# A layer kernel on one core: a second fold in its Fourier mixing, output projection and top-k in one stage, context rows gathered as quarter rows

## The reference

```
x = x + gate1 * (concat(fourier(p), retention(p)) @ w_out)    # p = modulated RMSNorm(x) @ w_in
h2 = RMSNorm(x) * (1 + scale2) + shift2
aff = softmax(h2 @ w_router)                                  # 16 experts
gates, idx = top_k(aff.T, cap)                                # 128 latent and 32 context tokens an expert
y = (silu(h2[idx] @ w_gate) * (h2[idx] @ w_up)) @ w_down      # 2816 hidden columns an expert
x = x + gate2 * scatter_add(gates * y)
```

## Time and profile before

| what | us |
|---|---|
| median of 3 runs (3186.18 to 3187.97) | 3187.58 |
| profiled execution | 3188.28 |
| its span | 3186.5 |
| PE busy in the span | 2995.0 (94%) |
| DVE, ACT, POOL busy | 1039.8, 692.7, 323.3 |
| mean granted clock of PE, as a share | 0.969 |

### The profile page before, as it was taken

The page is one execution under the profiler, slowest core; times in us unless marked ns, Lnnn a source line. Parts: engine busy times, 40 slices in busy tenths (PEclk is TensorE's granted clock), DMA queues, the critical chain, the costliest instruction groups (busy, mean ns, idle before and its releaser), DMA issues. The chain is left out here.

```text
span 3186.5 us, 50737 instructions
## 1 busy us (share of the span) xinstructions
PE 2995.0 (94%) x20563; PEld 2622.7 (82%) x20563; DVE 1039.8 (33%) x1977; ACT 692.7 (22%) x1158; POOL 323.3 (10%) x436
## 2 busy tenths in 40 slices
PE   5899998897499999999999999999999999999994
PEld 1899997586488888888888888888888888888883
DVE  4333331222533333333333333333333333333322
ACT  4222221233112121212212121212212121212212
POOL 1243330122000000000000000000000000000002
PEclk9999999898699999999999999999999999999997
DMA  9311102343577786868687786968787696968684
GB/s 372 99 41 35 40 12 66 106 145 134 166 245 248 232 289 202 295 207 287 229 275 251 228 293 198 295 207 290 228 273 255 224 294 199 294 208 292 220 270 147
DMA packets 483301, 668.17 MB, mean 210 GB/s; under 512 B 14689, under 2 KB 418993, under 8 KB 480050
## 3 DMA queue, kind: packets, MB, share of 16 engines
q1 hardware_dynamic: 476978, 644.45, 60.4%
q0 software_dynamic: 6144, 20.98, 2.8%
HBM read 633.39 MB, written 31.98 MB: 209 GB/s over the span
## 5 line engine op out<-in xcount | busy, mean ns | idle before, releaser
L1393 PEld LDWEIGHTS psG<-X,rawW 128*128 128x128 f32 x5632 | 772.5, 191 | 73.0 <-issue 72.1
L1393 PE MATMUL psG<-X,rawW 128*128 128x160 f32 x5632 | 815.0, 303 | 1.1 <-DVE X L1493 0.7
L1393 PE MATMUL psU<-X,rawW 128*128 128x160 f32 x5632 | 793.8, 299 | 0.0
L1393 PEld LDWEIGHTS psU<-X,rawW 128*128 128x128 f32 x5632 | 774.6, 190 | 0.0
L1474 ACT ACTIVATE wD_hi<-rawW 128x1024 fp32r<-128x1024 f32 x352 | 352.6, 1049 | 1314.1 <-PE psP L1412 1286.5
L1521 DVE TENSOR_TENSOR wD_lo<-rawW,wD_hi 128x1024 fp32r<-128x1024 f32 x352 | 415.2, 1220 | 560.0 <-ACT wD_hi L1474 560.0
L1526 DVE TENSOR_TENSOR hf<-sg,psU 128x320 f32<-128x320 f32 x176 | 85.9, 488 | 939.8 <-issue 825.7
L1407 PE MATMUL psS<-wD_hi,hid_hi 128*128 128x512 f32 x704 | 240.4, 423 | 0.0
L1407 PE MATMUL psS<-wD_hi,hid_lo 128*128 128x512 f32 x704 | 221.1, 395 | 0.0
L1407 PE MATMUL psS<-wD_lo,hid_hi 128*128 128x512 f32 x704 | 218.1, 391 | 0.0
L1550 POOL DMA_INDIRECT xgS<-xn,gi x16 | 16.4, 1024 | 1759.6 <-DVE gi L1518 1723.1
(11 more groups left out here) (219 smaller groups left out, 2720.7 us busy)
## 6 DMA issues: line engine op xcount, KB each, us to landing
rawW<-in_w_gate SPq DMA_DIRECT2D x176, 1024.0 KB, 7.8
rawW<-in_w_up SPq DMA_DIRECT2D x176, 1024.0 KB, 11.0
rawW<-in_w_down SPq DMA_DIRECT2D x176, 1024.0 KB, 5.3
wm<-in_w_mod SPq DMA_DIRECT2D x24, 1024.0 KB, 9.0
raw<-in_w_in SPq DMA_DIRECT2D x32, 192.0 KB, 2.5
rawc<-catT SPq DMA_DIRECT2D x10, 512.0 KB, 6.1
acc<-x SPq DMA_DIRECT2D x10, 512.0 KB, 2.7
xn<-xn SPq DMA_DIRECT2D x10, 512.0 KB, 4.1
```

Source lines behind the costliest of these rows:

```text
L1393: mm = pe.matmul(out[:, f, 0:C], w[:, k, f * P:(f + 1) * P], X[:, odd, k, :], start=(k == 0), stop=(k == NK - 1), skip_group_check=True)
```

## The change

In C the position DFT is folded a second time: `V` holds even and odd combinations of 256 positions, the tables shrink, and the matmuls into `pa` and `pb` have 256 columns; the one-row and single-column matmuls go, and a matmul of two columns (`edge`) gives what the fold leaves over. PE's loop is written out. SP loads `w_out`, `w_router` and half of the first two `catT` tiles during C.

D and E become one stage. PE transposes the residual stream without its norm; ACT copies it in one piece (`x1T`); the logits are made from `wrA` (router weight times scale) with 32 stationary columns in four column groups (`partials`), added up by `fold4`, and corrected by the norm's factor and a shift row (`srow`). The residual add moves from POOL to DVE, the scaling to `xn` from DVE to ACT. The softmax is done tile by tile (`affinity`), and DVE's rounds for the latent tokens start between tile 8's and tile 9's work.

The ring's first loads are issued at the start of F. In F the context rows are 128 quarter rows (`xgP`, `ysP` 128x256, on views `xn2q`, `accq`). The first expert's transposes go to eight banks (`first_x`), scaled by ACT and DVE in turn; later experts transpose `xgP` in one step only (`CTX_K`), and DVE then scales eight 128x32 pieces.

```diff
+                            for k in KO:
+                                sp.dma_start(rawo[:, k, :], io["w_out"][0, k * P:(k + 1) * P, :]).then_inc(d_raw[k], 16)
+                            for t in range(2):
+                                sp.dma_start(rawc[:, t, HALF[0], :], catv[:, HALF[0], t * P:(t + 1) * P]
+                                             ).then_inc(d_early[t], 16)
+                            sp.dma_start(wr[:], io["w_router"][0].rearrange("(k p) e -> p k e", p=P)).then_inc(d_wr, 16)
...
                     over_groups(sp, body)
                     store(H - 1)
-                    sp.wait_ge(c_out, 16 + 16 * H)
...
-                            pe.matmul(pa[:], Z[:, n, 0, :], pcos[:, n, 0:512], start=(n == 0), stop=False)
-                            pe.matmul(pb[:], Z[:, n, 1, :], psin[:, n, :], start=(n == 0), stop=(n == 3))
+                            pe.matmul(pa[:, at], Z[:, n, 0, :], pcos[:, t, odd, :], start=(t == 0), stop=(t == 1))
+                            mm = pe.matmul(pb[:, at], Z[:, n, 1, :], psin[:, t, odd, :], start=(t == 0), stop=(t == 1))
+                        mm.then_inc(c_lat, 1)
                         pe.wait_ge(c_rowc, g + 1)
-                        pe.matmul(pa[:], Zrow[:], palt[:, 0:512], start=False, stop=True)
-                        for n in range(4):
-                            pe.matmul(pm[:, 256:257], Z[:, n, 0, :], pcos[:, n, 512:513], start=(n == 0), stop=False)
-                        pe.matmul(pm[:, 256:257], Zrow[:], palt[:, 512:513], start=False, stop=True)
...
+                        act.wait_ge(c_lat, g + 1)
+                        act.activation(Bs[:].rearrange("p a k -> p (a k)"), pb[:], ACT.Copy).then_inc(c_bs, 1)
+                        waits(act, (c_rowc, g + 1), (c_out, 16 * (g + 1)))
+                        act.activation(yf[:, 512:513], zc[:, 1:2], ACT.Copy, scale=N_S ** -0.5)
                         act.wait_ge(c_pos, g + 1)
...
+                        dve.tensor_tensor(V[:, 0, 0, :], Ue[:, 0:256], Ue[:, 512:256:-1], ALU.add).then_inc(c_part, 1)
+                        dve.tensor_tensor(V[:, 0, 1, :], Ue[:, 0:256], Ue[:, 512:256:-1], ALU.subtract)
+                        dve.tensor_tensor(V[:, 1, 0, 1:256], Uo[:, 1:256], Uo[:, 511:256:-1], ALU.subtract)
+                        dve.tensor_tensor(V[:, 1, 1, 1:256], Uo[:, 1:256], Uo[:, 511:256:-1], ALU.add)
+                        dve.tensor_copy(V[:, 1, 1, 0:1], Uo[:, 256:257])
+                        dve.tensor_copy(edge[:, 0:1], Ue[:, 256:257])
+                        waits(dve, (c_part, 2 * g + 1))
+                        dve.tensor_reduce(part2[:].unsqueeze(2), V[:, 0, 0, :].rearrange("p (m a) -> p a m", a=2), AX.X,
+                                          ALU.add).then_inc(c_part, 1)
+                        waits(dve, (c_part, 2 * g + 2))
+                        dve.scalar_tensor_tensor(edge[:, 1:2], part2[:, 0:1], Ue[:, 256:257], part2[:, 1:2],
+                                                 ALU.add, ALU.subtract).then_inc(c_fold, 1)
...
+                        waits(dve, (c_bs, g + 1), (c_rowc, g + 1), (c_out, 16 * (g + 1)))
+                        dve.scalar_tensor_tensor(As[:], alt[:], zc[:, 0:1], pa[:, 0:256], ALU.mult, ALU.add).then_inc(c_as, 1)
+                        dve.tensor_tensor(yf[:, 1:512:2], pa[:, 256:512], Bs[:, 1, :], ALU.add)
+                        dve.tensor_tensor(yf[:, 1023:512:-2], pa[:, 256:512], Bs[:, 1, :], ALU.subtract)
+                        waits(dve, (c_as, g + 1))
+                        dve.tensor_tensor(yf[:, 0:512:2], As[:], Bs[:, 0, :], ALU.add)
+                        dve.tensor_tensor(yf[:, 1022:512:-2], As[:, 1:256], Bs[:, 0, 1:256], ALU.subtract).then_inc(c_yd, 1)
...
-                                mm = pe.matmul(lg[:, 0:E], h2T[:, 1 - slot, k, :], wr[:, k, :], start=(k == 0),
...
-                                mm = pe.transpose(trs[:, k * P:(k + 1) * P], xn[:, slot, k * P:(k + 1) * P], ident[:])
...
+                                mm = pe.matmul(lg[:, r * E:(r + 1) * E], modT[:, 3, k, r:r + 1].broadcast_to([P, P]),
+                                               wr[:, k, :], start=(k == 0), stop=(k == NK - 1))
...
+                            mm = pe.transpose(trs[:, k * P:(k + 1) * P], x1[:, t % 2, k * P:(k + 1) * P], ident[:])
...
+                            j = k % 4
+                            mm = pe.matmul(lg[32 * j:32 * j + 32, 0:P], wrA[:, req(t), k, :], x1T[:, k, :],
+                                           start=(k < 4), stop=(k >= 4), skip_group_check=True)
...
+                        pe.matmul(lg[:, P:P + E], parts[:], fold4[:], start=True, stop=True).then_inc(d_lg, 1)
...
+                            if kk % 4 == 0:
+                                pe.wait_ge(d_clo, 2 * n + kk // 4 + 1)
...
+                                shift_rows()
+                            if n and kk == 2:
+                                transposes(n - 1)
+                            if n and kk == 3:
+                                partials(n - 1)
+                            if n and kk == 4:
+                                logits(n - 1)
+                            if n == TS and kk == 6:
+                                pe.wait_ge(d_aff, TS)
+                                for t in range(TS // 2):
+                                    tr = pe.transpose(tb[0:48, t * P:(t + 1) * P], affS[:, t, :], ident[:])
+                                tr.then_inc(e_tb, 1)
...
+                    gate_rows(ops[0], 0, 3)
+                    transposes(T - 1)
+                    gate_rows(ops[1], 1, 4)
+                    partials(T - 1)
+                    logits(T - 1)
...
-                                op = act.activation(h2T[:, slot, k, :], trs[:, k * P:(k + 1) * P], ACT.Identity,
...
+                    for t in range(T):
+                        if t + 2 < T:
+                            split(t + 2, 0)
+                            split(t + 2, 1)
+                        act.wait_ge(d_x1, t + 1)
+                        act.activation(sq[:], x1[:, t % 2, :], ACT.Square, accum_out=ss[:, t:t + 1]).then_inc(d_sq, 1)
+                        act.wait_ge(d_tr, t + 1)
+                        act.activation(x1T[:].rearrange("p k t -> p (k t)"), trs[:], ACT.Copy).then_inc(d_xT, 1)
+                        act.wait_ge(d_rs, t + 1)
+                        if t >= 2:
+                            act.wait_ge(d_st[t % 2], 32 * (t // 2))
+                        act.activation(xn[:, t % 2, :], x1[:, t % 2, :], ACT.Copy, scale=rs[:, t:t + 1]).then_inc(d_xn, 1)
+                        act.wait_ge(d_part, t + 1)
+                        act.activation(parts[:], lg[:, 0:P], ACT.Copy).then_inc(d_parts, 1)
+                        act.wait_ge(d_sub, t + 1)
+                        act.activation(L[:, t, :], L[:, t, :], ACT.Exp, accum_out=sm_[:, t:t + 1]).then_inc(d_exp, 1)
+                    act.wait_ge(d_bc, 3)
...
+                        dve.tensor_tensor(x1[:, t % 2, :], ops[t % 2][:], gate1[:, r, :], ALU.mult).then_inc(d_gx, 1)
+                        dve.wait_ge(d_gx, t + 1)
+                        dve.wait_ge(d_x[t % 2], 16 * (t // 2 + 1))
+                        dve.tensor_tensor(x1[:, t % 2, :], x1[:, t % 2, :], xt[:, t % 2, :], ALU.add).then_inc(d_x1, 1)
+                        if t + 2 < T:
+                            split(t + 2, 0)
...
+                        dve.scalar_tensor_tensor(L[:, t, :], lg[:, P:P + E], rs[:, t:t + 1], srow[:, r, :],
+                                                 ALU.mult, ALU.add).then_inc(d_lc, 1)
+                        dve.wait_ge(d_lc, t + 1)
+                        own(dve.tensor_reduce(mx[:, t:t + 1], L[:, t, :], AX.X, ALU.max))
+                        dve.tensor_scalar(L[:, t, :], L[:, t, :], mx[:, t:t + 1], None, ALU.subtract).then_inc(d_sub, 1)
+                        dve.wait_ge(d_exp, t + 1)
+                        own(dve.reciprocal(sm_[:, t:t + 1], sm_[:, t:t + 1]))
...
+                    dve.wait_ge(e_tb, 1)
+                    dve.tensor_copy(top[0:48, :], tb[0:48, :]).then_inc(e_top, 1)
+                    dve.wait_ge(e_top, 1)
+                    rounds(0, 1)
+                    residual(TS)
+                    rounds(1, 3)
+                    affinity(TS)
+                    rounds(3, 5)
+                    residual(TS + 1)
+                    rounds(5, 8)
+                    affinity(TS + 1)
+                    rounds(8, 9)
...
+                        if t == 1:
+                            gp.wait_ge(d_bc, 2)
+                            gate_diag(5)
...
+            first_x = [psG[0][:, 0, 0:CS], psG[1][:, 0, 0:CS], psU[0][:, 0, 0:CS], psU[1][:, 0, 0:CS],
+                       psS[:, 0, 0:CS], psS[:, 1, 0:CS], psX[:, 0, 0:CS], psP[:, 0:CS]]
...
+                    for i in range(RING):
+                        for kind in (G_, U_, D_):
+                            if i == 0 and kind == D_:
+                                sp.wait_ge(f_got, 32)
```

(106 more changed lines are left out.)

520 lines of the change are left out of this document (205 added, 315 removed).

## The result

The changed kernel takes 3076.31 us (median of 4 runs, 3075.35 to 3078.3) against 3186.88 for the kernel before in the same comparison: a ratio of 0.9654, 95% interval 0.9637 to 0.967. The forecast was 3108, with a range of 3081 to 3133: the direction was right, the size was not. The profiled execution took 3075.88 us, its span 3074.1, that is 112.4 less than the span before; the forecast's sum was 79.8.

What follows compares the result with a forecast made beforehand. PE, busy for 94% of the span, was taken to bound the kernel, with thin or idle places in C, D, top-k and F's start. Stage savings summed to -79.8 us, giving 3108; own range 3094 to 3122, with rivals 3081 to 3133.

Steps and rivals of the forecast that it cites:

- Expert steps: F, 15 experts: eight small transposes go and two large come in each, 14.4 to 26 us less; -18 taken.
- The sum to D's tile 1: From the span's start through C and D's first tile: -25.9 us, of -21.6, -4.0 and -0.3.
- the 3.3 given back: In C: PE's waits for DVE, whose new fold is longer, return 3.3 us of the saving.
- D's first tile: Start of D: PE starts earlier, but DVE's weight splits pace it; 26.3 us instead of 26.6, -0.3.
- D and E: Tile 1's start to first indices: tiles of 12.77 us, top-k rounds begun before the last tile's work; -31.7 us.
- Rival (1): D's tiles stay long: partials cost 1.70 us and catT's load comes late; +14, 3122 us, chance 0.18.
- (4): The top-k does not move: D and E save 12 us instead of 32; 3128 us, chance 0.04.
- F's start: First indices to first gate matmul: 14.4 us instead of 18.1, -3.7 (12 to 17).
- The tail: End of F: ysP with 256 columns is cheaper, its scatter has four times the rows; -0.5 us.
- Rival (2): More saved: steps -8, F's start -2.4, clock in D's first tile -3, partials -2; 3092 us, chance 0.16.
- Rival (3): Quarter rows are slow: first gather and last scatter in F cost 3 us each; 3114 us, chance 0.07.
- Rival (5): Slower: ring not filled during the top-k, so the weights' stream decides in F; 3190 us or more, chance 0.02.

Runs made afterwards that it cites:

- the experiment: The changed kernel with the loads of w_out, w_router and the first halves of catT at D's start instead of during C: 3094.44 us.

## Why the prediction was wrong

**Expert steps: the term that failed.** The step read "The small transpose takes 0.17, the large one 0.20", from the spacing of starts in the earlier trace rows, and took -18, "nearer to the row of the transpose itself". The runs put 0.35 to 0.40 on the small one and 0.11 on the large one: seven steps that save 0.39 and one that saves 0.19 are 2.9 us an expert, 44 for 15, and F from the first gate to the last context matmul shows 45.4. Two things were misread. The 0.20 behind the large transpose was already the small one's wait for its load: `PEld` stood idle for 0.19 there, which the rows of PE alone don't show. And the 0.51 of the earlier trace rows, the honest price of both, was split by halves as a bound, where the trace had steps with two and steps with none but none with one. What the small transpose costs is the change of shape around it, a mechanism that the sum did not have. The Trainium skill (TensorEngine Tiling (Array Packing), Key Properties) states that changing the tiling mode drains TensorE. The traces agree, with 0.31 to 0.40 us for a change there and back. The prediction did not weigh that rule, though it bears on this change.

**The sum to D's tile 1** was right (-27.3 for -25.9), partly by luck. `mix(0)` took 9.2 us with its wait, D began 1.6 us after PE's last matmul (1.5), and the slow `cdft` was a low clock, as read: 0.54 of full speed over its 3.59 us. But the sum did not have the low clock in `project(1)`, 0.50 from 510.8 to 513.8 us, which cost 1.5; less waiting in C (1.5 us instead of the 3.3 given back) and a second slow `cdft` in `mix(1)` before (2.73 us) made up for it. D's first tile took 26.4 us (26.3) by another way: DVE's splits did not pace PE, which worked without a wait from 593.91 us until tile 1's, its first 12 matmuls at a clock of 0.50. That the loads during C matter more than the first matmul's delay, only the experiment showed.

**D and E** were right: tiles of 12.86 (12.77), partials of 0.64 (0.7), indices 35.4 us after tile 9 (38.1). Tile 9 took 0.7 us more than the others, with a wait of 0.1 instead of 1.0; the affinity took 1.5 us instead of 2.4 each time. Rival (1), a long tile, did not come, nor did (4).

**F's start** was right in sum (13.7 for 14.4), but by other parts, so by luck: the gather was slower (9.3 for 7.0), and transposes and scalings were faster (4.4 for 7.4, with all transposes in 2.4 us and the eight small scalings in 1.83, partly side by side). **The tail**, from the last context matmul on, gave -0.9 (-0.5).

**Rival (2)**, more saved, had the right sign and is too small (3092). Of its four parts only the first came, the dearer small transpose, and it took that at half of 0.51; F's start took 13.7 us and not 12, the clock in D's first tile was not kept up, and the tiles were not cheaper. **Rival (3)**, slow quarter rows, is refuted: without weights beside it the gather's rows reach PE 6.4 us after the indices, as whole rows did before (6.5), and the tail got shorter. The rule on small transfers quoted there does not set the time of this kernel. **Rival (5)**, the stream: from the first gate matmul on PE waits for no weights. The upper end of the forecast's own range, 3122, does not come out of its two bounds, which give 3116; nothing hangs on it.

## What to carry to other kernels

Price an instruction on TensorE by the difference between stretches with and without it, from one fixed instruction to the next, not by the spacing of its own starts; and look at the weight loads' timeline beside the matmuls', where a load that starts with its matmul instead of ahead of it shows a break. Keep stationaries of one shape together: pad a small one to the full shape, or collect the small ones of several steps. Each change there and back cost 0.3 to 0.4 us here; over the 176 steps, changes added or taken out made 29 to 60 us.

## What the runs showed of the hardware that was not expected

Full transposes with three quarters zeros beat small ones by 0.30 us each. In these traces PE's loads start ahead of their matmul between stationaries of one shape, and stop for 0.19 to 0.41 us where the shape changes; the price is nearly the same for a change of height (0.35 to 0.40) and of width (0.31 to 0.36). Two gathers took 9.3 us beside 2 MB of weights and 6.4 alone. In `project(1)` a wait of 1.92 or 2.35 us was followed by 3 us at the lower clock (1.2 GHz, a granted 0.50 in the changed kernel), and one of 1.80 in the kernel before was not; neither the loads of `w_out` beside it nor the fold's place settles why, and it stays open.
